# Pair work of an RWKV-7 mixer moved between its receptance slots, and three rows of x made before the first weight split

## What is computed

```python
xr, xw, xk, xv, xa, xg = [h + xx * mu[c] for c in range(6)]
r = xr @ w_rkv[0]; k = xk @ w_rkv[1]; v = xv @ w_rkv[2]
w = -softplus(-(w0 + tanh(xw @ w1) @ w2)) - 0.5
decay = exp(-exp(w)); a = sigmoid(a0 + (xa @ a1) @ a2); g = sigmoid(xg @ g1) @ g2
kk = (k * k_k) per head / max(norm, 1e-12); k = k * (1 + (a - 1) * k_a)
S = S * decay + (S @ -kk) (kk*a)^T + v k^T; y = S @ r      # step by step
bonus = sum(r * k * r_k) * v; o = ((groupnorm(y) * ln_w + ln_b) + bonus) * g; out = o @ w_o
```

## Time and profile before

| | |
|---|---|
| time, median of 3 runs | 1461.51 us (1460.57 to 1462.02) |
| the profiled execution | 1460.54 us, span 1458.8 us |
| mean granted clock of TensorE | 0.973 |
| PE busy | 1392.3 us (95%) |
| PEld busy | 1350.0 us (93%) |
| DVE busy | 857.1 us (59%) |
| ACT busy | 584.8 us (40%) |
| DMA | 188.98 MB, mean 130 GB/s |

### The profile page before, as it was taken

The page is one execution under the profiler, slowest core; times in us unless marked ns, Lnnn a source line. Parts: engine busy times, 40 slices in busy tenths (PEclk is TensorE's granted clock), DMA queues, the critical chain, the costliest instruction groups (busy, mean ns, idle before and its releaser), DMA issues.

```text
span 1458.8 us, 28480 instructions
## 1 busy us (share of the span) xinstructions
PE 1392.3 (95%) x11742; PEld 1350.0 (93%) x11742; DVE 857.1 (59%) x1294; ACT 584.8 (40%) x757; POOL 14.0 (1%) x28
## 2 busy tenths in 40 slices
PE   5999999698799998999999999999999999999997
PEld 5999999686689986899999999999999999999997
DVE  4555544776869366665555555555456867555543
ACT  5333333477344333353333344333333235333332
POOL 0000000300000000000000000000000000000000
PEclk9999999898799899899999999999999999999999
DMA  5333334232125211144443454443444444444342
GB/s 224 130 140 137 135 128 148 103 118 87 59 71 170 73 42 62 58 145 144 144 146 131 145 180 146 145 144 117 148 167 145 145 145 145 144 148 156 126 145 98
DMA packets 44220, 188.98 MB, mean 130 GB/s; under 512 B 15888, under 2 KB 17296, under 8 KB 28016
## 3 DMA queue, kind: packets, MB, share of 16 engines
q1 hardware_dynamic: 44144, 187.89, 37.5%
HBM read 182.65 MB, written 5.22 MB: 129 GB/s over the span
## 4 chain that ended last, share of the span: by engine, by line
PE 90%; DVE 4%; ACT 3%; issue 2%; POOL 1%; DMA 1%; SPq 0%; ACTq 0%; DVEq 0%
PE psum L335 48%; PE psum L367 22%; PE psum L811 5%; PE psum L505 4%; ACT w_hi L246 1%; PE psum L1046 1%; PE psum L997 1%; PE psum L972 1%; PE psum L883 1%; PE psum L1066 1%; DMA w_raw<-in_gu 1%; PE psum L1030 1%; PE psum L897 1%; PE psum L1015 1%; PE psum L1079 1%
## 5 line engine op out<-in xcount | busy, mean ns | idle before, releaser
L251 DVE TENSOR_TENSOR w_lo<-w_raw,w_hi 128x2048 fp32r<-128x2048 f32 (+1 forms) x188 | 388.4, 2066 | 238.4 <-ACT w_hi L246 238.0
L335 PE MATMUL psum<-x_hi,w_hi 128*128 128x322 f32 (+2 forms) x1600 | 499.9, 312 | 19.1 <-DVE x_lo L298 17.5
L246 ACT ACTIVATE w_hi<-w_raw 128x2048 fp32r<-128x2048 f32 (+1 forms) x188 | 326.0, 1734 | 459.0 <-PE psum L335 227.0
L335 PE MATMUL psum<-x_hi,w_lo 128*128 128x322 f32 (+2 forms) x1600 | 500.6, 313 | 0.0
L335 PE MATMUL psum<-x_lo,w_hi 128*128 128x322 f32 (+2 forms) x1600 | 500.5, 313 | 0.0
L335 PEld LDWEIGHTS psum<-x_hi,w_hi 128*128 128x128 f32 x1600 | 303.8, 190 | 20.7 <-issue 17.3
L335 PEld LDWEIGHTS psum<-x_hi,w_lo 128*128 128x128 f32 x1600 | 302.7, 189 | 0.0
L335 PEld LDWEIGHTS psum<-x_lo,w_hi 128*128 128x128 f32 x1600 | 301.8, 189 | 0.3
L367 PE MATMUL psum<-h_hi,w_lo 128*128 128x322 f32 (+2 forms) x704 | 219.8, 312 | 0.0
L367 PE MATMUL psum<-h_lo,w_hi 128*128 128x322 f32 (+2 forms) x704 | 219.2, 311 | 0.0
L367 PE MATMUL psum<-h_hi,w_hi 128*128 128x322 f32 (+2 forms) x704 | 218.8, 311 | 0.0
(11 more groups left out here) (206 smaller groups left out, 1366.1 us busy)
## 6 DMA issues: line engine op xcount, KB each, us to landing
w_raw<-in_gu SPq DMA_DIRECT2D x88, 1024.0 KB, 4.8
w_raw<-in_down SPq DMA_DIRECT2D x64, 704.0 KB, 4.1
w_raw<-in_mix SPq DMA_DIRECT2D x16, 1024.0 KB, 4.8
w_raw<-in_scin SPq DMA_DIRECT2D x12, 1024.0 KB, 4.7
w_raw<-in_wo SPq DMA_DIRECT2D x4, 1024.0 KB, 4.8
w_raw<-in_scout SPq DMA_DIRECT2D x4, 1024.0 KB, 4.8
s<-in_wkv SPq DMA_DIRECT2D x8, 256.0 KB, 3.4
out_wkvs<-s SPq DMA_DIRECT2D x8, 256.0 KB, 2.0
```

The costliest lines, as they stand in the source:

```text
L246: act.activation(whi[par][:, :tiles * P], raw[par][:, :tiles * P], ACT.Copy).then_inc(hi_ready, 1)
L251: dve.tensor_tensor(wlo[par][:, :n], raw[par][:, :n], whi[par][:, :n].bitcast(F32), ALU.subtract).then_inc(lo_ready, 1)
L335: last = pe.matmul(PS[:, banks[j], :n], w[:, (2 * k + j) * P:(2 * k + j + 1) * P], v[:, k, :n], start=(k == 0 and i == 0), stop=(k == KT - ...
```

## The change

1. Start: three rows of x are made before ACT and DVE split slot 0; slot 1 is split behind all eight. PE's wait for the constants moves to the norm's matmul.
2. The maximum, root and reciprocal of kk's norms are made earlier: the root ahead of the first sigmoid on ACT, the reciprocal after the fourth XR row on DVE. On ACT the split of slot 6 moves behind the last XR rows, that of slot 7 ahead of the last two a-groups, and the splits of slots 8 to 10 one pair earlier each.
3. The outer lora groups use four bank pairs. The receptance groups use banks 6, 0, 6, 0 and wait for `r_scaled` 2 and 4 from the third on; all couplings but the last share banks 2 and 3.
4. PE: spreads of 128 rows, 0 and 1 ahead of slot 6 and 2 to 7 between its row groups; couplings 0 between slots 8 and 9; then couplings, sums and turns in a written-out order.
5. DVE: all normalisations ahead of pair 0; in pair p also `r_decayed(p - 1)`, the mask of p - 3 and the rk product of p - 3 (temporary tiles 4 and 5). The XG rows come behind.
6. ACT: the exponentials for the chunk ends by pair; copies of turned tiles 0 to 2 ahead of the XG rows.

```diff
@@ open_group
-                if 2 <= g < R_GROUP + 2:
+                if 2 <= g < 6:
                     pe.wait_ge(mix_evac, g - 1)
-                elif g == R_GROUP + 3:
-                    pe.wait_ge(r_scaled, 2)
+                elif g == 7:
+                    pe.wait_ge(kk_max, 1)
+                elif 8 <= g < R_GROUP + 2:
+                    pe.wait_ge(mix_evac, (5, 6, 7, 8, 9, 10, 12, 13)[g - 8])
+                elif R_GROUP + 2 <= g < G_GROUP:
+                    pe.wait_ge(r_scaled, 2 * (g - R_GROUP - 1))
                 elif g == G_GROUP:
+                    pe.wait_ge(z_ready, 16)
                     pe.wait_ge(kv_turned, PAIRS)
@@ tables
-        BANKS.update({R_GROUP + i: b for i, b in enumerate((0, 2, 6, 0))})
+        BANKS.update({6 + i: b for i, b in enumerate((4, 6, 0, 2, 4, 6, 0, 2))})
+        BANKS.update({R_GROUP + i: b for i, b in enumerate((6, 0, 6, 0))})
-        Z_BANKS = (4, 6)
+        Z_BANKS = (2, 2, 2, 2, 2, 2, 2, 0)
@@ mix_pe
-            for p in range(PAIRS):
+            def couplings(p):
                 pe.wait_ge(a_scaled, p + 1)
                 pe.wait_ge(bk_scaled, p + 1)
-                pe.wait_ge(r_scaled, max(p + 1, 6 if p else 1))
-                if p >= 2:
-                    pe.wait_ge(z_ready, 2 * p - 2)
+                pe.wait_ge(r_scaled, p + 1)
+                if p == 0:
+                    pe.wait_ge(mix_evac, 14)
+                elif p < PAIRS - 1:
+                    pe.wait_ge(z_ready, 2 * p)
+                else:
+                    pe.wait_ge(r_scaled, PAIRS)
...
+            spread(0)
+            spread(1)
+            project(6, XR, True, between=lambda k: spread(k + 2) if k + 2 < PAIRS else None)
+            project(7, XR, False)
+            project(8, XR, False)
+            couplings(0)
+            project(9, XR, False, True)
+            couplings(1)
+            couplings(2)
+            sum_rk(0)
...
@@ mix_act
+            act.wait_ge(kk_max, 1)
+            act.activation(tmp[3][0:HEADS, :T], tmp[3][0:HEADS, :T], ACT.Sqrt).then_inc(kk_root, 1)
             for s in range(4):
                 x_hi_tile(XR, 2 + s)
...
+            for p in range(5, PAIRS):
+                x_hi_tile(XG, p - 3)
+                keep_bk(p)
@@ mix_dve
+            for p in range(PAIRS):
+                a_norm(p)
+                if p == 4:
+                    split(7)
+            dve.wait_ge(mix_evac, 10)
+            dve.wait_ge(bk_padded, 1)
+            for p in range(PAIRS):
+                if p in (1, 3, 5):
+                    split(8 + p // 2)
+                pair_front(dve, p)
+                if p >= 1:
+                    pair_back(dve, p - 1)
+                    r_decayed(p - 1)
+                if p >= 3:
+                    take_z(p - 3)
+                    take_rk(p - 3)
...
+            split(11)
+            dve.wait_ge(rk_sum, PAIRS - 1)
+            mixed(XG, 2)
+            dve.wait_ge(rk_sum, PAIRS)
+            mixed(XG, 3)
@@ scalar, at the start (vector alike)
-            for par in range(2):
-                split_act(act, 0, par, BIG, slot_used, 2)
             for m in range(KT):
+                if m == 3:
+                    split_act(act, 0, 0, BIG, slot_used, 2)
                 res_act(act, 0, m, m % 2, m >= 2)
+            split_act(act, 0, 1, BIG, slot_used, 2)
```

More of the change, by code:

```diff
@@ L799, in open_group, with project @@
                 return BANKS[g]
-            def project(slot, ver, fresh, final=False, shift=0):
+            def project(slot, ver, fresh, final=False, shift=0, between=None):
                 pe_slot_wait(pe, MIXB + slot)
@@ L814, in project @@
                         last.then_inc(x_used, 1)
+                    if between and k < KT - 1:
+                        between(k)
                 last.then_inc(mix_out, 1)
@@ L858, in spread @@
                     pe.wait_ge(a_normed, p - 1)
-                pe.matmul(PS[:, 4 + p % 2, :T], con[0:HEADS, K_SELT + P * p:K_SELT + P * p + P], rstd[0:HEADS, :],
+                elif p == 0:
+                    pe.wait_ge(kk_inv, 1)
+                    pe.wait_ge(mix_evac, 11)
+                pe.matmul(PS[:, 4 + p % 2, :T], con[:, K_SELT + P * p:K_SELT + P * p + P], rstd[:, :],
                           start=True, stop=True).then_inc(kk_spread, 1)
[L862 to L868, removed]
             def sum_rk(p):
@@ L882, in turn_bk @@
                         rows = slice(HD * hh, HD * hh + HD)
-                        last = pe.matmul(PS[rows, 2 + c // 8, (c % 8) * HD:(c % 8 + 1) * HD],
+                        last = pe.matmul(PS[rows, 6 + c // 8, (c % 8) * HD:(c % 8 + 1) * HD],
                                          bk[rows, p, c, :, :].rearrange("p h t -> p (h t)"),
@@ L900, in mix_pe @@
                 last.then_inc(z_done, 1)
[L901 to L907, removed]
+            spread(0)
[8 more added lines that the diff above has]
+            sum_rk(0)
+            couplings(3)
+            sum_rk(1)
+            couplings(4)
+            sum_rk(2)
+            couplings(5)
+            sum_rk(3)
+            turn_bk(0)
+            turn_bk(1)
+            couplings(6)
+            sum_rk(4)
+            turn_bk(2)
+            couplings(7)
+            sum_rk(5)
+            turn_bk(3)
+            turn_bk(4)
+            sum_rk(6)
+            turn_bk(5)
+            turn_bk(6)
+            sum_rk(7)
+            turn_bk(7)
             project(10, XG, True, True)
@@ L1176, in decay, with ends @@
                 act.activation(tmp[6 + p % 2][:, RD], sw[:, p, PAD:], ACT.Exp, scale=E_HALF).then_inc(decays, 1)
+            def ends(p):
+                for lo, hi, first, step in ((0, PCHUNKS, C - 1, C), (PCHUNKS, PCHUNKS + SEQS, PCHUNKS * C + STEPS - 1, STEPS)):
+                    act.activation(dend[:, p, lo:hi], sw[:, p, first:first + (hi - lo - 1) * step + 1:step], ACT.Exp,
+                                   scale=-E_HALF).then_inc(ends_ready, 1)
             def decay_r(p):
@@ L1236, in mix_act @@
             split(11)
[L1237 to L1244, removed]
+            keep_bk(3)
+            keep_bk(4)
+            for p in range(5, PAIRS):
+                x_hi_tile(XG, p - 3)
+                keep_bk(p)
+            for k in range(5, KT):
+                x_hi_tile(XG, k)
             act.wait_ge(rk_sum, PAIRS)
-            act.activation(rks[:, :], PS[0:HEADS, 0, :T], ACT.Copy).then_inc(rk_kept, 1)
+            act.activation(rks[:, :], PS[0:HEADS, 4, :T], ACT.Copy).then_inc(rk_kept, 1)
             x_hi(XV)
```

113 lines of the change are left out of this document (56 added, 57 removed).

## The result

The changed kernel takes **1469.95 us** (median of 5 runs, 1467.69 to 1472.35) against 1461.51 for the kernel before (1459.68 to 1462.06): ratio 1.0063, 95% interval 1.0052 to 1.0074, so it is 8 us slower. The forecast was 1469. The profiled execution of the changed kernel took 1471.9, its span is 1470.1.

A forecast was written before the change was run, and what follows sets the result against it. PE was taken to bound the dense stages, leaving the start and the mixer's pair work, where DVE waits for couplings, to change. Sum: 1461.5 - 2.5 (start) + 10 (mixer) = 1469 us, range 1458 to 1476.

The forecast's parts named there:

- Start: Kernel's start: first rows hide weight loading, first matmul at 15.0 instead of 17.4; -2.5 us, bounds -1.5 and -3.
- The slots' start, and its gain spent: Receptance slots: first dense matmul at 339.5 instead of 344.1, but interleaved spreads let DVE begin pair 0 only at 350.0 (before 349.0).
- The decisive wait: Mixer's pair loop: mask 1 needs couplings behind slot 9, released in DVE's pair 4; DVE idle about 11 us.
- Slot 8 takes 9.0: Receptance slot 8 after some 5 us of idle PE: half clock, 9.0 us, ending at 372.9.
- I expect slot 10 to start at half clock, 1.5 more: End of the mixer: PE idle between turns, so slot 10 starts at half clock, costing 1.5 us more.
- The 128-row spreads stream the same 336 columns: Spreads around slot 6: wider rows, same columns, so the edit goes at nothing.
- The tail: Mixer's last couplings, sums, turns and copies: end at 434.5 against 425.7 before, +9; 1.8 us before turn 7.
- 1 (full clock): Slots 8, 9, 10 and tail: clock stays at 1.00, mixer costs 2, time 1461; chance 0.18.
- 2 (DVE doesn't stand): Mixer: DVE does not stand for slot 9 and PE becomes the bound, 26 us earlier, time 1433; chance 0.06.
- 5 (one bank pair): Mixer: shared banks expose couplings, masks of pairs 2 to 6 wait 1.4 us each, time 1476; chance 0.03.
- 3: Mixer: small work runs at half clock, mixer +17, time 1476; chance 0.13.
- 4: Kernel's start does not move, slot 1 or x being late; time 1471.5; chance 0.06.

The follow-up runs named there:

- couplings 0 early: Changed kernel with the couplings of pair 0 ahead of receptance slot 8 instead of behind it; 1462.64 us, ratio 1.0015 to the kernel before.
- both: Changed kernel with two moves in PE's order: couplings 0 ahead of slot 8, couplings 1 and 2 ahead of slot 9; 1456.72 us, ratio 0.9966.
- fillers: Changed kernel with six matmuls, results never read, ahead of slot 8 and six ahead of slot 9 to keep PE busy; 1467.84 us, ratio 1.0035.
- sum 0 early: Changed kernel with couplings 0 ahead of slot 8, couplings 1, 2 and the rk sum of pair 0 ahead of slot 9; 1454.44 us, ratio 0.9951.
- splits later: Run with couplings 0 to 2 and rk sum 0 moved ahead and turns and sums reordered, plus DVE's splits of slots 8 to 10 one pair later; 1442.44 us.

## Why the prediction was right

**Start.** Forecast -2.5, measured -3.06 in the trace (slot 1 at 25.12, 28.18 before) and -2.5 in the medians of the run with the start alone. The first matmul came at 14.71 for 15.0.

**The slots' start, and its gain spent.** On the clock of the trace before, the first spread came at 334.21 + 3.06 = 337.3, as forecast, the first dense matmul at 339.4 (339.5). Pair 0 began at 350.9 for 350.0. The root starts 0.01 us after its table load in the new trace too (load at 320.94, 1.28 long, root at 322.23).

**The decisive wait** is where it was put, and its price is shown: 4.8 us for pair 0 (forecast 3.5), 11.9 for pair 1 (about 11), PE idle 5.4 and 5.2 ahead of the slots (some 5). The two moves of PE's order take 13.2 us back.

**Mis-sized terms.** "Slot 8 takes 9.0" and slot 9 the same: they took 10.1 and 10.3, since the nearest row was a slot that had been at half clock for a shorter part; 2.4 us short. Pair 0 was another 0.9 late. The other way, couplings 5 are let end at 410.5 in the prediction, 2.1 behind mask 4, where its own price for them is 1.4. "I expect slot 10 to start at half clock, 1.5 more" did not happen: slots 10 to 14 (240 matmuls) took 37.2 us, as with the start alone. The gaps alone do not decide that: the same stretch took 38.6 to 39.3 in four of the other runs (couplings 0 early, both, fillers, sum 0 early), where turn 7 was wholly or partly at half clock, behind the same two gaps of PE (1.88 ahead of turn 7, 1.1 ahead of slot 10). So the mixer cost 12.5 in the trace for 10, and 11.5 in the medians. That the total came within 1 us is in part luck: the slots and pair 0 were 3.3 short, and about half of that was made up by a loss at slot 10 that did not come.

**A term right by luck.** "The 128-row spreads stream the same 336 columns" was written at nothing. The columns are the same, and the edit is nonetheless worth 10.1 us (1480.08 against 1469.95). The forecast had assumed that slot 6 gets its full clock back soon, without asking what would bring it back; with narrow spreads the kernel would have been outside the range.

**The tail** behaved as laid out. The path through the sum of pair 7, DVE's row 3 and copy 6 cost 1.88 before turn 7 (forecast 1.8), and turned out to be a matter of order, worth 5 us with the earlier turns.

**Rivals.** 1 (full clock) fell at its own condition, slots of 10 us; the fillers, which gave slot 9 its full clock and slot 8 a part of it, were worth 2.1 us in the medians and 5.2 at slot 10, not 8. 2 (DVE doesn't stand) fell likewise; with the waits taken away and the tail and splits reordered the kernel reaches 1442, not 1433. 5 (one bank pair) needed over 1 us of waiting at each mask, and DVE waited for none of masks 2 to 4 and 0.5 for mask 5; its 3.5 and 1.9 before masks 6 and 7 are for couplings queued behind turns. Of 3, only couplings 3 and 5 ran at half clock (2.61 and 2.58 against 1.50), the turns at full. 4 fell with the first matmul.

**What the banks cost.** The shared pair of banks makes PE wait for DVE, rather than DVE for PE: 10.1 us in four waits for masks, of which the last lies on the chain. PE had done couplings 4 and sum 2, and the inputs of couplings 5 were ready, when it stood still until mask 4 had read the banks:

```profile
408.33 2.58 PE L908 MATMUL psum<-ar,bk 64*64 64x64 f32 x44 [2.71 <-DVE z L1509]
```

The prediction's sum holds this wait, as "couplings 5 follow mask 4". The rule of the Trainium skill (Perfetto Trace Analysis, Matmuls) that independent groups rotate through different banks, so that emptying one overlaps the next, bears on it, and on slots 8 and 9 as well: they stand still 5.4 and 5.2 us because DVE has not yet emptied banks 6 and 0. No run gave couplings or receptance groups another pair, so what that would be worth stays open. The runs show that with the banks as they are the order alone takes back 13.2 us.

## What to carry to other kernels

When a big matmul group is released by an engine's step n and the engine's next step needs a small matmul queued behind that group, the engine stands for the whole group whatever its speed; put the small ones ahead of the big one, and every small one on which that engine depends, the sums that free its buffers too. Count where a freed wait turns up next before pricing the removal: here the sum behind slot 9 came to light only when the couplings had moved ahead of it. Before calling an edit free because its columns are the same, look at the granted clock around it.

## What the runs showed of the hardware

The granted clock of a stretch in which PE was busy without a gap depended on the rows of the small matmuls in it. Two fp32 passes of 16 rows and 336 columns after every six dense ones kept the clock at 0.50 for 20 us and more; the same with 128 rows rose to 1.00 about 6 us after the first spread. Ahead of the output projection eight spreads of 16 rows, waiting for DVE in between, ran at 0.50 from 1.8 us after the first on, those of 128 rows at 1.00 throughout, with PE busy 3.1 to 3.4 of 5 us. The Trainium skill (TensorE: Matmul & The Clock Gate, Why this matters for your kernels) says that a matmul over 32 rows takes the time of one over 128; for 16 rows the trace agrees at an equal clock (the first four passes took 2.57 and 2.58 us), and the clock is where the two part. The length of a gap without matmuls alone does not tell the clock behind it. Slot 8 or 9 began at full clock after 1.0, 1.6 and 1.7 us (splits later, fillers, couplings 0 early) and at half clock after 1.5 and 1.9 us (sum 0 early, both) and after 5.2 and 5.4. After 2.0 us (fillers) and 3.1 us (spreads of 16 rows) slot 8 began at full clock and fell to half 1.3 and 0.9 us later.
